# A two-layer block on one Trainium2 core: matmuls behind a residual read x times the norm weight, and the token roots are applied when products leave PSUM

## The reference, cut to what matters

```
# end of the first layer's mixer, then its feed-forward part
x = x + merged @ w_out
h = rmsnorm(x, norm_ffn_g)                  # x * rsqrt(mean(x*x) + eps) * g
u = causal_dwconv(h @ w_up, conv_ffn_w)     # 3 taps along the tokens
x = x + (silu(u[..., :2816]) * u[..., 2816:]) @ w_down
x = rmsnorm(x, norm_final_g)                # end of the first layer
# start of the second layer: a second norm straight on top of the first
h = rms_norm(x, norm1_g)
z, xbc, dt_raw, q, k, v, g_ssd, g_att = split(h @ w_in)
...                                         # SSD branch, window attention, w_out
x = x + merged @ w_out
h2 = rms_norm(x, norm2_g)
x = x + hier_moe(h2, ...)                   # 64 experts in 8 groups, top 2
```

## Time and profile before

| | |
|---|---|
| time of the kernel before, 3 runs | 1538.26 us median (1537.3 to 1538.49) |
| the profiled execution | 1537.22 us, span 1535.5 us |
| PE busy | 1456.7 us, 95% of the span |
| DVE, ACT busy | 517.2 us (34%), 335.5 us (22%) |
| granted PE clock, mean | 0.993 |
| bytes moved by DMA | 347.38 MB, mean 226 GB/s |

### The profile page before, as it was taken

One profiled execution on the slowest core, in us unless ns is written; L12 is line 12 of the kernel. 1 busy time (PEld: TensorE's weight loads), 2 busy tenths in 40 slices (PEclk: granted clock), 3 DMA queues, 4 the chain that ended last, 5 costly groups with the idle time before them and its releaser, 6 DMA issues.

```text
span 1535.5 us, 29276 instructions
## 1 busy us (share of the span) xinstructions
PE 1456.7 (95%) x12702; PEld 1232.8 (80%) x12702; DVE 517.2 (34%) x1262; ACT 335.5 (22%) x738; POOL 6.7 (0%) x72
## 2 busy tenths in 40 slices
PE   8999999999999999899999999997999989998886
PEld 6868889978888888788888888887777777776665
DVE  0536164221344330207862542013333322222222
ACT  2153411341100000112455531102111111111111
POOL 0000000000000000000000000000000000000000
PEclk9999999999999999999999999998999999999999
DMA  8333424224344323544333443474999999999995
GB/s 327 131 138 124 145 92 154 83 83 149 131 159 151 134 76 151 202 139 164 133 115 124 151 165 114 150 328 176 390 424 423 424 424 424 424 424 423 424 424 235
DMA packets 58334, 347.38 MB, mean 226 GB/s; under 512 B 12416, under 2 KB 13536, under 8 KB 18656
## 3 DMA queue, kind: packets, MB, share of 16 engines
q1 hardware_dynamic: 55536, 339.20, 56.9%
q10 hardware_dynamic: 2672, 6.33, 1.2%
HBM read 413.21 MB, written 1.49 MB: 270 GB/s over the span
## 4 chain that ended last, share of the span: by engine, by line
PE 89%; DMA 6%; issue 2%; ACT 1%; DVE 1%; SPq 0%; DVEq 0%; ACTq 0%
PE bank L389 38%; PE bank L1036 9%; PE bank L440 9%; PE bank L403 6%; PE bank L1056 5%; PE bank L1067 4%; PE bank L1080 4%; DMA scratch<-w_down_e_dram 2%; PE bank L456 2%; DMA ring<-w_gate_e_dram 2%; DMA work<-w_gate_e_dram 2%; PE bank L545 1%; PE bank L501 1%; PE bank L914 1%; PE bank L365 1%
## 5 line engine op out<-in xcount | busy, mean ns | idle before, releaser
L389 PE MATMUL bank<-hT,ring 128*128 128x256 f32 x2080 | 455.7, 379 | 3.4 <-DVE hT L1672 3.4
L389 PEld LDWEIGHTS bank<-hT,ring 128*128 128x128 f32 x2080 | 393.0, 190 | 60.5 <-issue 8.3
L1681 DVE TENSOR_TENSOR xT<-xT,bank 128x512 f32<-128x512 f32 x100 | 68.8, 688 | 319.2 <-PE bank L1056 205.7
L389 PE MATMUL bank<-work,ring 128*128 128x256 f32 x640 | 139.5, 379 | 0.0
L389 PEld LDWEIGHTS bank<-work,ring 128*128 128x128 f32 x640 | 121.3, 190 | 17.2 <-issue 1.0
L440 PE MATMUL bank<-work,ring 128*128 128x256 f32 x608 | 131.6, 379 | 0.0
L440 PEld LDWEIGHTS bank<-work,ring 128*128 128x128 f32 x608 | 115.5, 190 | 15.7
L1036 PE MATMUL bank<-work 128*32 128x128 f32 x2144 | 113.6, 273 | 10.3 <-issue 9.2
L1036 PEld LDWEIGHTS bank<-work 128*32 128x32 f32 x2144 | 103.8, 110 | 22.2 <-issue 22.0
L403 PE MATMUL bank<-ring,hT 128*128 128x256 f32 x448 | 98.5, 380 | 1.6 <-DVE hT L1672 1.6
L403 PEld LDWEIGHTS bank<-ring,hT 128*128 128x128 f32 x448 | 84.4, 190 | 13.7 <-issue 2.6
(11 more groups left out here) (336 smaller groups left out, 1653.8 us busy)
## 6 DMA issues: line engine op xcount, KB each, us to landing
work<-w_up_e_dram SPq DMA_DIRECT2D x33, 1024.0 KB, 23.7
work<-w_down_e_dram SPq DMA_DIRECT2D x33, 1024.0 KB, 25.9
work<-w_gate_e_dram SPq DMA_DIRECT2D x30, 1024.0 KB, 25.7
ring<-w_gate_e_dram SPq DMA_DIRECT2D x26, 1024.0 KB, 26.3
ring<-w_down_e_dram SPq DMA_DIRECT2D x23, 1024.0 KB, 25.7
ring<-w_up_e_dram SPq DMA_DIRECT2D x23, 1024.0 KB, 26.1
ring<-w_up_dram SPq DMA_DIRECT2D x22, 1024.0 KB, 4.9
ring<-w_gates_dram SPq DMA_DIRECT2D x20, 1024.0 KB, 4.9
```

Source lines behind the costliest of these rows:

```text
L389: m = mm(b[:, j * SEQ:(j + 1) * SEQ], w[:, k, j * P:(j + 1) * P], tile(k), start=(k == 0), stop=(k == kt - 1))
L1681: return v.tensor_tensor(dst, a, b, ALU.add)
```

## The change

Nothing in the mathematics changes. A root per token can be pulled out of a product over features, because it is the same for every feature.

1. `residual` also writes `gainT`, x times the norm weight, one pair behind each added pair. The first two `up1` products and all six `att2` products, with `dt`, read `gainT`, so that they need no root.
2. The sum of squares is made whole by the vector engine (all four pairs, then halves), and PE's part is one matmul with ones (`summed_norm`), put behind `up1` 0 at joint A and behind `att2` 0 at joint B.
3. `hT` is made from `gainT` and the root in 4 pieces (`normed_hidden`), for `up1` 2 and later, and for `xbc` 8 and later.
4. `up1` 0 and 1 are multiplied by the root while they are copied out of their banks (`scaled`), and are then convolved from there. `att2` is scaled by a token root at eviction, two ACT instructions of 256 columns in place of one of 512; `dt` likewise on the vector engine.
5. At joint B ACT also squares x times the final norm's weight (`sq2`). Both sums go through one bank (`norms2`). With S1 the mean square of x and S2 that of x times the final gain, log1 = log(S1 + eps), log2 = log(S2 / (S1 + eps) + eps), and the product of both roots is exp(-0.5 (log1 + log2)). ACT (L1484 to L1491 of the changed kernel) and the vector engine (from `square1_ready` to `token_roots`) hand this back and forth. The final norm itself is written to `xT` later, in 8 pieces behind `dt`.

The core of the diff:

```diff
+        gainT, sq2 = area(19968, KD, SEQ), area(17920, 2048)
+            def summed_norm(key, sums):
+                b = new(key)
+                pe.wait_ge(bank_free(key), used(key) - 1)
+                pe.wait_ge(S("squares_summed"), nth("squares_summed"))
+                for n, a in enumerate(sums):
+                    m = mm(b[:, n * SEQ:(n + 1) * SEQ], ones, a[:, 0:SEQ], start=True, stop=True)
+                m.then_inc(product_ready, 1)
+
+            def each_gained(k):
+                if k % 2 == 0:
+                    pe.wait_ge(S("gained"), nth("gained"))
...
-            norm_sum("norm_ffn", summed=True)
             for i in range(KF):
-                to_features(("up1", i), "w_up", hT, fresh=each_normed if i == 0 else None)
+                if i == 2:
+                    pe.wait_ge(S("h_ready"), 1)
+                to_features(("up1", i), "w_up", gainT if i < 2 else hT, fresh=each_gained if i == 0 else None)
+                if i == 0:
+                    summed_norm("norm_ffn", [sq])
             for i in range(4):
                 split_features(("down1", i), "w_down", ffT, KF // 2, 2, fresh=each_ff if i == 0 else None)
-            norm_sum("norm_final", summed=True)
-            norm_sum("norm1")
             for i in range(6):
-                to_tokens(("att2", i), "w_att2", hT, fresh=each_normed if i == 0 else None)
+                to_tokens(("att2", i), "w_att2", gainT, fresh=each_gained if i == 0 else None)
                 if i == 0:
+                    summed_norm("norms2", [sq, sq2])
                     pe.wait_ge(S("late_loads"), nth("late_loads", 48))
-                    small_features("dt", w_dt, hT)
+                    small_features("dt", w_dt, gainT)
                 if i == 1:
                     small_tokens("dt")
+            pe.wait_ge(S("h_ready"), 2)
...
-            squares_of_x(lambda i: act.wait_ge(bank_free("down1", i), used("down1", i)))
-            root("norm_final")
-            squares_of_x(lambda i: act.wait_ge(S("x_new"), nth("x_new", 2)))
-            root("norm1")
+            for i in range(4):
+                act.wait_ge(bank_free("down1", i), used("down1", i))
+                A_(sq[:, 512 * i:512 * i + 512], xT[:, 2 * i:2 * i + 2, :].rearrange("p k t -> p (k t)"), ACT.Square)
+                for k in (2 * i, 2 * i + 1):
+                    m = A_(sq2[:, SEQ * k:SEQ * k + SEQ], xT[:, k, :], ACT.Square, scale=col("norm_final", k))
+                m.then_inc(S("squares"), 1)
...
-                A_(qkv_tok[:, :, i * 256:(i + 1) * 256], at("att2", i)[:, :].rearrange("p (t n) -> p t n", t=TT),
-                   ACT.Copy).then_inc(bank_free("att2", i), 1)
+                for t in range(TT):
+                    m = A_(qkv_tok[:, t, i * 256:(i + 1) * 256], at("att2", i)[:, t * 256:(t + 1) * 256], ACT.Copy,
+                           scale=token_root[:, t:t + 1])
+                m.then_inc(bank_free("att2", i), 1)
...
             def residual(name, squared, gains, sums):
                 for i in range(4):
...
+                    dve.wait_ge(bank_free(name, i), used(name, i))
+                    for k in (2 * i, 2 * i + 1):
+                        m = ts(gainT[:, k, :], xT[:, k, :], gains(k))
+                    m.then_inc(S("gained"), 1)
                     if i == 2:
-                        sum_squares(squared)
+                        sum_squares(squared, sums)
+                dve.wait_ge(S("squares"), squared + 4)
...
+            def normed_hidden(root):
+                for i in range(4):
+                    m = mul(hT[:, 2 * i:2 * i + 2, :], gainT[:, 2 * i:2 * i + 2, :], rep(root, 2, SEQ))
+                m.then_inc(S("h_ready"), 1)
...
-            residual("out1", 4)
-            norm("norm_ffn", hT, "normed")
+            residual("out1", 4, lambda k: col("norm_ffn", k), [sq])
+            dve.wait_ge(S("rs_ready"), nth("rs_ready"))
+            normed_hidden(rs[:, 0, 0:SEQ])
+            scaled = (rs[:, 1, :], tmp[:, 0, :])
```

More of the change, by code:

```diff
@@ L254, in build @@
         qk_r = sm2[:, 160:200]
+        gains12, token_root = sm2[:, 200:208], sm2[:, 208:210]
         ridx = sb("ridx", [P, TT, 16], U32)
@@ L351, in unit_read, with norm_sum @@
                 unit_product[-1] = len(product) - 1
-            def norm_sum(key, summed=False):
+            def norm_sum(key):
                 b = new(key)
[L356 to L362, removed]
+                for k in range(KD):
                     if k % 2 == 0:
@@ L966, in _ @@
             route_pair(3)
-            pe.wait_ge(S("squares"), nth("squares", 4))
+            pe.wait_ge(S("squares"), nth("squares", 12))
             for k in (6, 7):
@@ L1692, in norm, with conv @@
                     stt(dst[:, k, :], xT[:, k, :], col(gain, k), rs[:, 0, 0:SEQ]).then_inc(S(done), 1)
-            def conv(key, i, taps, name, into=None, shift=None):
+            def conv(key, i, taps, name, into=None, shift=None, src=None):
                 dve.wait_ge(product_ready, made(key))
@@ L1948, in gated, with residual @@
                 mul(merged[:, pair, :], quads(at((first, i))[:, :], 2), gA[:, pair, :]).then_inc(bank_free(first, i), 1)
-            def residual(name, squared):
+            def residual(name, squared, gains, sums):
                 for i in range(4):
@@ L1983, in _ @@
                     dve.wait_ge(S("ff"), nth("ff"))
-                conv(("up1", i), i, 3, "conv_ffn")
+                if i < 2:
+                    dve.wait_ge(product_ready, made("up1", i))
+                    mul(quads(scaled[i], 2), quads(at(("up1", i))[:, :], 2), rep(rs[:, 0, 0:SEQ], 2, SEQ))\
+                        .then_inc(S("dve_step"), 1)
+                    dve.wait_ge(S("dve_step"), nth("dve_step"))
+                conv(("up1", i), i, 3, "conv_ffn", src=scaled[i] if i < 2 else None)
                 if i >= 1:
@@ L1987, in _ @@
             ffn_product(KF - 1)
-            residual("down1", 8)
-            norm("norm_final", xT, "x_new")
-            norm("norm1", hT, "normed")
+            mul(gains12, col("norm_final", 0, 8), col("norm1", 0, 8)).then_inc(S("dve_step"), 1)
+            dve.wait_ge(S("dve_step"), nth("dve_step"))
+            residual("down1", 8, lambda k: gains12[:, k:k + 1], [sq, sq2])
+            dve.wait_ge(S("square1_ready"), 1)
+            mul(tmp[:, 0, 0:SEQ], at("norms2")[:, SEQ:512], rs[:, 0, SEQ:512]).then_inc(bank_free("norms2"), 1)
+            dve.wait_ge(S("log2_ready"), 1)
+            add(tmp[:, 0, SEQ:512], rs[:, 0, 0:SEQ], rs[:, 1, 0:SEQ]).then_inc(S("logs_added"), 1)
+            dve.wait_ge(S("root12_ready"), 1)
+            root12 = rs[:, 1, SEQ:512]
+            mul(quads(tmp[:, 0, 0:SEQ], 2), quads(root12, 2), rep(ident, 2, P)).then_inc(S("dve_step"), 1)
+            dve.wait_ge(S("dve_step"), nth("dve_step"))
+            v.tensor_reduce(token_root, quads(tmp[:, 0, 0:SEQ], 2), AX.X, ALU.add).then_inc(S("token_roots"), 1)
+            normed_hidden(root12)
+            dve.wait_ge(S("root1_ready"), 1)
+            dve.wait_ge(S("token_roots"), 1)
             dve.wait_ge(product_ready, made("dt"))
             v32 = lambda ap: ap.rearrange("p (t n) -> p t n", t=TT)
-            add(v32(dt_), v32(at("dt")[:, 0:64]), rep(row("dt_bias2"), TT, 32)).then_inc(bank_free("dt"), 1)
+            for t in range(TT):
+                m = stt(dt_[:, t * 32:(t + 1) * 32], at("dt")[:, t * 32:(t + 1) * 32], token_root[:, t:t + 1],
+                        row("dt_bias2"), ALU.mult, ALU.add)
+            m.then_inc(bank_free("dt"), 1)
             dve.wait_ge(bank_free("dt"), used("dt"))
@@ L2003, in _ @@
             stt(v32(dA), v32(dt_), -1.0, rep(expA2, TT, 32)).then_inc(S("dA"), 1)
+            for k in range(KD):
+                stt(xT[:, k, :], xT[:, k, :], col("norm_final", k), rs[:, 0, 0:SEQ])
             dve.wait_ge(S("qk_squares"), nth("qk_squares"))
@@ L2157, in _ @@
                 if i == 2:
-                    sum_squares(16)
+                    sum_squares(12, [sq])
+                    add(sq[:, 0:SEQ], sq[:, 0:SEQ], sq[:, SEQ:512]).then_inc(S("squares_summed"), 1)
             both = range(TT)
```

38 lines of the change are left out of this document (28 added, 10 removed).

## The result

The changed kernel takes 1524.06 us (median of 4 runs, 1521.97 to 1525.64), the kernel before in the same comparison 1537.78 us (4 runs, 1536.32 to 1538.49): ratio 0.9895, 95% interval 0.9875 to 0.9915. Forecast were 1522.8 us, range 1520.4 to 1526.2. Measured twice more, the ratio was 0.9900 (0.9883 to 0.9918) and 0.9886 (0.9870 to 0.9903). The ratio is an estimate of its own and not the quotient of the two medians, which is 0.9911 here: by the medians the change gives 13.7 us, by the ratio 16.1 us (13.1 to 19.2), and the forecast 15.5 lies within that interval. The profiled execution of the changed kernel took 1525.64 us, the slowest of its four, with a span of 1524.0 us.

The account below looks back on a forecast made before the run. PE was taken to bound the kernel until the experts' load stream starts, which hangs on PE; loads bound it after. Savings of 3.93 + 11.56 = 15.49 us took 1538.26 to 1522.8 us, range 1520.4 to 1526.2.

Parts of the forecast that it names:

- joint A: From the last `out1` eviction into `up1`: 4.36 us removed, one matmul of 0.43 added, net 3.93 us saved.
- joint B: From the end of `down1` to `att2` 0: 12.42 us removed, two sum matmuls of 0.86 added, net 11.56 us saved.
- that case: At joint A without PE's second covering product: the `hT` pieces would cost 2.8 us plus two copies of 0.69.
- Edits costed at nothing: Split `att2` evictions, final norm pieces, gain pieces and sums during `down1`, bank rotation: 0.2 us together at most.
- The sum, 15.49 us: Savings of 3.93 us at joint A and 11.56 us at joint B, taken off the time before.
- The signs: Profile after: no idle before `up1` 0 or `att2` 0, no lower clock near 640, no `h_ready` wait, restart near 1060.6.
- rival 1: In the router, before the load stream starts, the clock falls out otherwise: 1520.6 or 1525.0 us; chance 0.12 beyond 1521.5 to 1524.
- My likeliest case: Whole kernel at 1521.5 to 1524 us, given a chance of 0.68.
- Rival 2: At the joints a new wait partly replaces the old, giving back some 2 to 4 us: 1525 to 1527; chance 0.10.
- Rival 3: The experts' load stream takes the gain: 1538.3 us if its start does not follow PE, 1530.5 if half; chance 0.04.
- Rival 4: Unbroken PE load from 402 to 1050 us lowers the clock; at 0.95 it costs 32 - 15.5, 1555 us; chance 0.02.
- Rival 5: `up1` 0 still waits for the root, so joint A gives nothing: 1526.7 us; chance 0.02.

Follow-up runs that it names:

- e4: Changed kernel plus 28 extra unused 128x256 matmuls (12.1 us of PE work) ahead of `att2` 0 at joint B; 1535.29 us, ratio 0.9962.
- e5: Changed kernel plus the same 28 unused matmuls, two in each of 14 rounds of the experts' stage; 1521.75 us, ratio 0.9878.
- e6: Changed kernel with only `up1` 0, not `up1` 0 and 1, running on `gainT` at joint A; 1529.93 us, ratio 0.9934.
- e2: Changed kernel with only joint B in the new form, joint A as before the change; 1529.07 us, ratio 0.9935.
- e3: Changed kernel, but at joint B PE waits for `hT` before `att2` 0, sums still made together, no scaling at eviction; 1535.32 us, ratio 0.9971.

## Why the prediction was right

- *What bounds the kernel.* This held. The runs e4 and e5 together show that PE's time counts ahead of the restart and not behind it.
- *Joint A, 3.93 us.* The table gives 4.00. The pieces of `gained` 3 ended 1.34 us after the eviction began, forecast 1.36. For `h_ready` the four pieces took 2.50 us, below the 2.8 to 3.3 that I bounded from single additions, and 3.3 us were to spare where 3.0 was forecast. The run e6 shows that the cover was named rightly: without it the stop is 3.7 us. The price for that case was too low. I wrote 2.8 us plus two copies, but the copies don't lie on PE's path, while the logarithm and the exponential do; and I left out what the clock costs behind a stop, 1.6 us.
- *Joint B, 11.56 us.* The table gives 11.45. `squares_summed` came 4.28 us after the eviction began (637.04) where 4.5 was forecast, the token roots 11.45 us after it (forecast 11.5), and the last piece of `hT` 13.9 (forecast 14.3). Two rows erred the other way, well within the margins: ACT's two scaled squares took 0.89 us and not 0.84, and an `att2` eviction in two 0.84 and not 0.77.
- *Edits costed at nothing.* The two stretches come out 0.07 above and 0.11 below their terms, so nothing of size is hidden there.
- *The sum, 15.49 us.* The table gives 15.45 for the part that the change touches. The medians of the three comparisons give 13.7, 14.8 and 16.1 us (the last against 1539.47), and their ratios 16.1, 15.4 and 17.5, each with an interval of some 3 us to either side that takes in 15.5. So the mechanism and the size are shown by the stretches; that a first median of four runs came within 1.3 us of the forecast is in part luck, because the untouched stretches scatter by 3.3, 1.6 and 2.7 us from profile to profile.
- *The signs.* All that were to be seen at the joints were seen: no idle time ahead of either first product, the clock at 1.00, `h_ready` never waited for. One sign of being wrong did show: the restart moved by 12.59 us, not by what the joints give. The cause lies in stretches that the change doesn't touch. The sign was badly chosen, because it compares two single executions.
- *The step that was too sure.* "Three runs lie within 1.2 us" was my reason against rival 1. With 23 and 10 runs the kernel before spans 1536.3 to 1543.9 and 1539.2 to 1544.2, so three runs said little about the spread. My likeliest case, 1521.5 to 1524, was too narrow for that, and 1524.06 lies just outside; the whole range was not.
- *A reading that was too coarse.* For joint A and for the long load I went by the page's slices, which can't show a fall of a few us. The windows bear both readings out: from 397 to 412 us the kernel before is at 1.00, and so is the changed kernel from 401 to 1034.
- *The rivals.* Rival 1, the clock in the router, is real but smaller than I priced it. In the first profile the gather stayed at 6.02 us; in the second and third of the changed kernel its 32 records took 5.62 and 5.54, and over the twelve profiles without the router's edit 5.17 (e2) to 6.47 us (e3), against 2.2 us to either side in the prediction. The row alone would have kept it at 5.99. The Trainium skill, TensorE: Matmul & The Clock Gate, section on the HAM clock gate, says that the gate's windows run free of the program, so that the same work can meet a rise or fall at another point. The traces agree with that: the gather differs as above, and the same 16 records at joint B took 5.38 and 6.51 us. Rival 2, a new wait, did not come: between 401 and 1040 us the list of PE's waits has one of 0.2 us, in the router, which the change leaves alone. Rival 3 is refuted by e4 and e5. Rival 4, the clock in the long run, is refuted by a mean of 1.00 over 633 us with 0.14 us idle; its price at 0.95 was slightly too low, since 648 / 0.95 - 648 is 34 us and not 32. Rival 5 is refuted by the timeline.

## What to carry over

Where a matrix product waits for a normalisation, ask whether the scale can be applied at its output: what counts is the work that the engine gets to do in the wait, here a product of 6.91 us against walks of 4 to 12 us, and not how short the walk to the root is made (e3: 0.4 to 1.5 us for the shorter walk, 11 for the cover). Count how many products the walk needs and check the margin of the last one; one too few at joint A turned a gain of 4.0 into a loss of 1.3 us. When medians disagree with the sum, cut the profiles at marks common to all kernels: here the touched stretches repeat to 0.01 us in profiles of the same kernel, and carry the answer that 2 to 3 us of scatter elsewhere blur.

## What the runs showed of the hardware

A stop of PE can cost more than its length. Behind 3.7 us of idle the clock stood at 0.68 to 0.75 and cost 1.6 us more (e6); behind 4.5 and 3.7 us in e3 it cost 2.7 (1.0 in the sums, 1.7 in the product). I had counted that only for joint B of before, where it is in the row. Short stops can do it too, and the same stop does not cost the same each time: behind 1.7 to 2.1 us near 197 us the clock fell in 3 of 12 executions, and behind 1.5 and 0.3 us near 338 us in 5 of 14. Matmuls whose results nobody uses, put into such a wait, can keep the clock up: the gather of 32 records went from 6.02 to 3.84 us, and the stretch with it became 1.3 to 2.9 us shorter. That the whole kernel becomes faster by it is likely and not shown clear of noise.
